# A hybrid pooling and window-attention layer: the MLP of three blocks as seven half-size products

## The reference

```python
n = rmsnorm(x)
h = x + (sig(gp) * pool(n) + sig(ga) * (attn(n) @ w_attn_up)) @ w_out   # the mixer
h = h + square(relu(rmsnorm(h) @ w_up)) @ w_down                        # the MLP, width 4096
y = rmsnorm(h)
```

## Time and profile before

| | |
|---|---|
| time, median of 3 runs | 2447.85 us (2447.26 to 2447.87) |
| span of the profiled execution | 2446.3 us |
| PE busy | 2423.0 us, 99% |
| DVE busy | 1328.5 us, 54% |
| ACT busy | 789.8 us, 32% |
| POOL busy | 173.1 us, 7% |
| DMA | 237.20 MB, 97 GB/s over the span |

### The profile page before, as it was taken

The page is one execution under the profiler, slowest core; times in us unless marked ns, Lnnn a source line. Parts: engine busy times, 40 slices in busy tenths (PEclk is TensorE's granted clock), DMA queues, the critical chain, the costliest instruction groups (busy, mean ns, idle before and its releaser), DMA issues.

```text
span 2446.3 us, 32439 instructions
## 1 busy us (share of the span) xinstructions
PE 2423.0 (99%) x12933; PEld 2055.9 (84%) x12933; DVE 1328.5 (54%) x1712; ACT 789.8 (32%) x1258; POOL 173.1 (7%) x168
## 2 busy tenths in 40 slices
PE   8999999999999999999999999999999999999997
PEld 8999999999977888888887788888887788888885
DVE  7645644445675564543576556445467555544444
ACT  4533322222443332222335334222243434222222
POOL 1400000000131000000024000000003400000000
PEclk9999999999999999999999999999999999999998
DMA  4223332222232333333332233332334233333231
GB/s 164 75 77 99 118 92 87 86 86 88 90 126 71 105 127 95 95 94 94 95 129 75 84 109 125 94 95 93 94 94 131 63 94 103 95 95 94 94 94 61
DMA packets 72248, 237.20 MB, mean 97 GB/s; under 512 B 8784, under 2 KB 9136, under 8 KB 72144
## 3 DMA queue, kind: packets, MB, share of 16 engines
q1 hardware_dynamic: 67408, 227.00, 30.0%
q10 hardware_dynamic: 4736, 8.75, 0.9%
HBM read 226.97 MB, written 8.85 MB: 96 GB/s over the span
## 4 chain that ended last, share of the span: by engine, by line
PE 99%; DVE 0%; DMA 0%; ACT 0%; DVEq 0%; issue 0%; SPq 0%; ACTq 0%
PE prod L335 95%; PE auxB L335 1%; PE auxA L439 1%; PE auxB L470 1%; PE auxB L453 1%; PE auxA L335 0%; DVE hT L774 0%; DMA raw<-weights 0%; DVE acc L756 0%; PE auxA L409 0%; DVE wL L728 0%; ACT wH L527 0%; DVE nL L762 0%; DVE acc L750 0%; DVE hT L944 0%; ACT acc L554 0%
## 5 line engine op out<-in xcount | busy, mean ns | idle before, releaser
L527 ACT ACTIVATE wH<-raw 128x1024 fp32r<-128x1024 f32 (+1 forms) x424 | 439.4, 1036 | 1530.3 <-PE prod L335 1526.7
L335 PE MATMUL prod<-nH,wH 128*128 128x512 f32 (+1 forms) x2320 | 747.1, 355 | 8.2 <-DVE nL L762 8.2
L335 PE MATMUL prod<-nL,wH 128*128 128x512 f32 (+1 forms) x2320 | 741.6, 352 | 0.0
L335 PE MATMUL prod<-nH,wL 128*128 128x512 f32 (+1 forms) x2320 | 741.4, 352 | 0.0
L728 DVE TENSOR_TENSOR wL<-raw,wH 128x1024 fp32r<-128x1024 f32 (+1 forms) x424 | 520.2, 1227 | 96.7 <-ACT wH L527 96.0
L335 PE MATMUL prod<-midL,wH 128*128 128x512 f32 (+1 forms) x1600 | 511.1, 352 | 0.0
L335 PE MATMUL prod<-midH,wL 128*128 128x512 f32 (+1 forms) x1600 | 511.1, 352 | 0.0
L335 PE MATMUL prod<-midH,wH 128*128 128x512 f32 (+1 forms) x1600 | 510.9, 352 | 0.0
L335 PEld LDWEIGHTS prod<-nH,wH 128*128 128x128 f32 x2320 | 407.9, 188 | 76.6 <-DVE wL L728 8.4
L335 PEld LDWEIGHTS prod<-nL,wH 128*128 128x128 f32 x2320 | 407.8, 188 | 61.2 <-issue 1.2
L335 PEld LDWEIGHTS prod<-nH,wL 128*128 128x128 f32 x2320 | 406.5, 188 | 60.6
(11 more groups left out here) (118 smaller groups left out, 1352.1 us busy)
## 6 DMA issues: line engine op xcount, KB each, us to landing
raw<-weights SPq DMA_DIRECT2D x392, 512.0 KB, 3.5
raw<-weights SPq DMA_DIRECT2D x32, 320.0 KB, 2.9
xT<-x SPq DMA_DIRECT2D x3, 2048.0 KB, 8.2
y<-hT ACTq DMA_DIRECT2D x12, 512.0 KB, 2.8
xT<-x SPq DMA_DIRECT2D x8, 272.0 KB, 5.3
y<-hT ACTq DMA_DIRECT2D x4, 544.0 KB, 2.8
rope<-tables SPq DMA_DIRECT2D x4, 512.0 KB, 4.4
cst<-consts SPq DMA_DIRECT2D x1, 96.0 KB, 6.6
```

The lines of the kernel that those rows point to most:

```text
L335: ins = nc.tensor.matmul(out[:, s, 0:hi - lo], lhs, rhs[:, lo:hi], start=first, stop=last)
L527: return nc.scalar.activation(out, in_, ACT.Copy, scale=scale)
```

## The change

Block 0 computes its MLP as before, but with two changes to who does what. In blocks 1 to 3 each product of the MLP is split in halves in its three dimensions (two halves of the tokens, of 256; two of the inputs, two of the outputs), and the 2x2x2 half-size block products, eight, are replaced by seven of sums of halves (one Strassen level in Winograd's form). A "token" in the code below is one such half-size product of one pair of output tiles `j` (tile j and tile j + 4) and one of seven kinds `r`: 4 input tiles, 3 matmuls each, of 256 columns, so 12 matmuls. A phase (an up or a down of one quarter) is 28 tokens, in the order of the table `ORDER`, and a block has 8 phases. The seven sums of the weights (four need arithmetic, three are the halves themselves) don't depend on the block. They are made in block 0 and kept in DRAM.

- **Block 0, new work.** For each of 32 pairs of units, POOL makes four 128x512 sums (`sum_weights`). In 5 of the 8 groups (`SPLIT_PHASES`; 20 pairs) ACT and DVE split three of the four sums (`sums_high`, `sums_low`, 128x1536 each), and SP stores 0.26 MB and 1.57 MB; in the others SP stores 1.05 MB. A place in `raw` is now also held until POOL has summed it, and POOL waits, before it writes one of two sets `wsum`, until the set's store has landed. ACT, not DVE, squares the hidden values now.
- **Blocks 1 to 3.** SP loads one half unit (0.26 MB) for a token, or a presplit sum (0.52 MB, high and low), which ACT and DVE needn't split. The hidden half blocks are put together from partial products by ACT copies, DVE additions and accumulation in PSUM (`up_step`); the down products are added to `hT` one by one (`down_step`), where they were added once per unit. The seven sums of the activations, too, are made and split by DVE and ACT (`gain_pair` in the mixer's last stage, `sum_T13` to `low2` in the MLP).

```diff
-                tt(work[:, 2, 0:n], work[:, m % 2, 0:n], work[:, m % 2, 0:n], ALU.mult).then_inc(hid_sq, 1)
+                    nc.scalar.activation(y, y, ACT.Square).then_inc(hid_sq, 1)
...
+ORDER = [(0, 1), (0, 5), (1, 1), (1, 5), (0, 2), (1, 2), (0, 6), (0, 3), (1, 6), (1, 3), (0, 7), (1, 7), (2, 5), (0, 4),
+         (2, 2), (1, 4), (2, 1), (3, 5), (3, 1), (3, 2), (2, 6), (2, 3), (3, 6), (3, 3), (2, 7), (3, 7), (2, 4), (3, 4)]
+SPLIT_PHASES = (0, 2, 4, 6, 7)
+def presplit(ph, pr):
+    return ph in SPLIT_PHASES and pr in (5, 6, 7)
...
+            def raw_place_free(*item):
+                for before in raw_free[item]:
+                    wait_split_low(sp, *before)
+                    if before[0] == "plain":
+                        wait(sp, s_S, before[2] // 2)
...
+            for n in range(2 * KD * NQ):
+                load_plain_unit(n)
...
+                if n % 2 and n >= 7:
+                    store_sums((n - 7) // 2)
...
+            def sum_weights(p):
...
+                if p >= 2:
+                    pool.wait_ge(set_out[p % 2], set_count[p - 2])
+                s = wsum[p % 2]
...
+                link(tt(s[:, 2, :], a11, a21, ALU.subtract))
+                link(tt(s[:, 1, :], s[:, 2, :], a22, ALU.subtract))
+                tt(s[:, 0, :], s[:, 1, :], a11, ALU.subtract)
+                tt(s[:, 3, :], a12, s[:, 1, :], ALU.add).then_inc(s_S.sem, 1)
...
+            def phase(b, ph):
+                every = (0, 1, 2, 3)
+                if ph % 2:
+                    for k in range(6):
+                        token(b, ph, k, (0, 1))
+                    for k in range(6):
+                        token(b, ph, k, (2, 3))
...
+                for kp in kps:
+                    if ph == 0 and k in (0, 4):
+                        wait(pe, s_gL2 if k == 0 else s_gL5, b, kp)
+                    if down and k in (0, 4):
+                        wait(pe, s_L5 if k == 0 else s_L2, b, q, kp)
+                    wh, wl = (wring[:, ring_slot(b, t), h, kp * P:(kp + 1) * P] for h in range(2))
+                    xh, xl = high[:, QUAD[r], kp, :], low[:, QUAD[r], kp, :]
+                    nc.tensor.matmul(out, wh, xh, start=kp == 0 and r in (1, 2, 5), stop=False, skip_group_check=True)
+                    nc.tensor.matmul(out, wh, xl, start=False, stop=False, skip_group_check=True)
+                    ins = nc.tensor.matmul(out, wl, xh, start=False, stop=kp == PAIRS - 1, skip_group_check=True)
...
+            def up_step(b, q, k):
+                if q == 0 and k == 6:
+                    invert("h", b)
+                    wait(dve, s_r, "h", b)
+                if k == 7:
+                    add_cb(b, q, 0)
+                    weights_ahead(b, 2 * q * NT7 + k)
+                    relu_z01(b, q, 0)
+                    return
...
+                if k in (10, 11):
+                    add_u3(b, q, k - 10)
+                    weights_ahead(b, 2 * q * NT7 + k)
+                    relu_z2(b, q, k - 10)
+                    return
...
+                if k == 27:
+                    sum_T13(b, q, 3)
+                    relu_z3(b, q, 3)
+                    sum_T2(b, q, 3)
+                    low5(b, q, 2)
+                    sum_T4(b, q, 2)
+                    low5(b, q, 3)
+                    sum_T4(b, q, 3)
+                    low2(b, q, 2)
+                    low2(b, q, 3)
+                weights_ahead(b, 2 * q * NT7 + k)
```

More of the change, by code:

```diff
@@ new lines, in build @@
+        rms, acc = own("rms", [P, CMAX]), own("acc", [P, CMAX])
+        kT = own("kT", [P, 2 * K_HALF + DEC])
+        vB = own("vB", [P, NT + 1, P])
+        cst = own("cst", [P, P + G * 16])
+        ones = own("ones", [P, P])
+        vec = own("vec", [P, 4 * KD + 6])
+        nsink = own("nsink", [P, 6])
+        eps_tile = own("eps", [P, 1])
+        columns = own("columns", [P, 7, 4])
+        carry, carry_s, state = (own(n, [P, G, 16]) for n in ("carry", "carry_s", "state"))
+        assert top[0] <= 229344
@@ L238, in wait @@
             eng.wait_ge(signal.sem, signal.count[item])
-        def unit_width(u):
-            return AO_WIDTH if u < M_MLP and MIXER[u][0] == "ao" else WIDTH
-        def wait_product(eng, b, i):
[L245 to L261, removed]
+        splits = []
@@ new lines, in raw_tokens, with ring_slot, wait_split_low, wait_raw @@
+        def raw_tokens(b, lo, hi):
+            return [t for t in range(lo, hi) if t < TOKENS and not is_split(b, t)]
+        def ring_slot(b, t):
+            return (t + SHIFT[b]) % RING
+        def wait_split_low(eng, *item):
+            eng.wait_ge(w_low, split_no[item])
+        def wait_raw(eng, *item):
+            eng.wait_ge(raw_in[raw_at[item]], raw_count[item])
+        def unit_width(i):
+            return AO_WIDTH if MIXER[i][0] == "ao" else WIDTH
+        def unit_row(b, i):
+            return MIXER.index(PLAN[b][i])
@@ L336, in stream, with three @@
                 return ins
-            def three(out, b, uslot, off, high, low, k, first, last):
-                wh, wl = wH[:, uslot, off:off + P], wL[:, uslot, off:off + P]
+            def three(out, b, wslot, off, high, low, k, first, last):
+                wh, wl = wslot[:, 0, off:off + P], wslot[:, 1, off:off + P]
                 stream(out, b, wh, high[:, k, :], first, False)
@@ L389, in before @@
                         sum_squares("f", b - 1)
-                product(b, i % 2, high, low, nk, before)
+                product(b, i, high, low, nk, before)
             def sum_squares(kind, b):
@@ L519, in _ @@
                     between(b, i)
-                quarters(pe, b, up, down, lambda b: down(b, NQ - 1))
+                if b == 0:
+                    for q in range(NQ):
+                        plain_up(q)
+                        plain_down(q)
+                else:
+                    for ph in range(PHASES):
+                        phase(b, ph)
             sum_squares("f", NB - 1)
@@ L621, in step @@
                     merged_high(b, m)
[L622 removed]
+                if kind == "out" and b == 0:
                     wait(act, s_h, b, m)
@@ new lines, in plain_down @@
+            def plain_down(q):
+                for i in range(KD):
+                    n = 16 * q + KD + i
+                    wait_plain(act, n)
+                    plain_split_ahead(n + 2)
+                    if q == NQ - 1:
+                        m = ORD[i]
+                        gained_high("x", 1, i)
+                        if i == 0:
+                            root("x", 1)
+                        act.wait_ge(down_added, hid(q, i))
+                        square("f", 0, i, hT)
+                        wait(act, s_sq, "f", 0, i)
+                        copy(hT[:, m, :], hT[:, m, :], g_fin[:, m:m + 1]).then_inc(s_fg.sem, 1)
+                    sums_high(n)
```

963 lines of the change are left out of this document (751 added, 212 removed).

## The result

| | before | after |
|---|---|---|
| time, median | 2447.86 us (2447.26 to 2447.99, 4 runs) | 2518.34 us (2515.88 to 2519.5, 4 runs) |
| span of the profiled execution | 2446.3 us | 2515.7 us |
| mean granted clock | 0.997 | 0.981 |

The ratio is 1.0286, with a 95% interval of 1.0273 to 1.0299: slower by 70.5 us, where 18 us less were forecast, and 38 us above the range. The page of after, beside the earlier trace rows: span and engines, the chain that ended last by engine and line, and the stores with their us to landing.

A forecast was written before the change was run, and what follows sets the result against it. PE was taken as the bound, without stalls at full clock: 2446.3 - 117.2 + 15.6 + 5.7 + 10.8 + 1.8 + 1.0 + 64.6 = 2428.6 us of span, so a median of 2430 us, range 2358 to 2480.

The forecast's parts named there:

- Ring: Block 0's MLP: POOL's sums, loads and stores wait in a circle, 15.4 and 13.2 us a pair against 12.02; +64.6 us.
- transfers: Loads and stores part of block 0's circle: 9.0 us in presplit pairs, 7.1 us in the others.
- second rival: Block 0: POOL and DVE block each other in each operation, eating the gain; 2482 to 2526 us; chance 0.22.
- Columns: MLP of blocks 1 to 3: 2688 matmuls of 256 columns at 118.15 ns replace 1536 at 232.21; -117.2 us.
- Weight load as a floor: Rival, blocks 1 to 3: 256 columns cost 125.28 ns like 272; 2476 us, or 2412 if block 0 keeps pace; chance 0.08.
- Turns: Up to down, 12 times: PE waits for DVE's relu (0.6 us) and `low5` (0.4), 1.3 us each; +15.6 us.
- Mixer to MLP: Join in blocks 1 to 3: token 4's weight split comes 1.9 us late behind DVE's sums, three times; +5.7 us.
- DVE at 90%: Up phases of blocks 1 to 3: DVE stays under PE's 39.7 us, at 90% or more, its work bunched.
- First and last quarter, handover: Reciprocal and root delay sums: +10.8 us in first quarters, +1.8 in last; handover to block 1 and end squares +1.0.
- the ring fits: Rival: loads and stores overlap, a pair stays under 12.02 us, block 0 keeps its length; 2366 us; chance 0.25.

The follow-up runs named there:

- experiment 2: Changed kernel with one more POOL subtraction in each of block 0's 32 pairs: 2560.33 us, +42.0 against the changed kernel.
- experiments 12 to 18: Seven runs on the kernel with earlier stores and both order changes (2377.25 us), shifting operand addresses or repeating weights: 2367.22 to 2377.09 us.
- experiment 9: Kernel before, each 512-column product of blocks 1 to 3 made as two of 256, first half's three instructions before the second's: 2481.50 us, +33.4.
- experiment 6: On top of experiment 1, `gain_low5` one product later, behind the next weight split, and ACT's high weights ahead of the gained halves: 2395.44 us, -20.2.
- experiment 5: On top of experiment 1, DVE makes `sum_T4` of pair 1 before `low5` in blocks 1 to 3: 2396.52 us, -19.1.
- experiment 1: Changed kernel with block 0's sums stored two weight loads earlier: 2415.66 us, 102.7 under the changed kernel, ratio to before 0.9869.
- 7 and 18: 7: experiment 5 and experiment 6 changes together on experiment 1, 2377.25 us. 18: 7 with weights placed 128 bytes higher against the moving columns, 2369.65 us.

## Why the prediction was wrong, step by step

- **Ring: the step that failed.** Its shape was right: loads that wait for sum p + 1, stores behind them, sum p + 2 behind the stores, with PE, ACT and DVE waiting in the order foreseen. Opening it gives 102.7 us back and lengthening it costs its full time. The size was 64.6. The term "transfers", 9.0 and 7.1 us, was too short: from the last sum to POOL's next start it took 11.3 us behind a store in two parts and 9.1 behind the others, on average. In the chain above it is 10.7 to the landing (407.7 to 418.4). SP's issues of 0.3 to 0.4 us each stand one after the other ahead of the store, and the DMA engines moved 184, 274, 209 and 293 GB/s in the four us from 409, where the forecast had 410 throughout, and only then 418 to 469. Why the first four were slow is not shown. POOL was priced too high, 6.4 and 6.1 for 5.7 and 5.3 us, which hid some of it. So the pairs came out at 17.0 and 14.4 us, for 15.4 and 13.2. Over 29 pairs POOL's starts are 15.9 us apart, 3.9 over PE's pace, or 113 us; forecast were 72 (17 x 3.4 + 12 x 1.2). About 10 us were taken by slack, near the 7.6 foreseen. The point of the second rival, 0.6 us a pair more than forecast, was passed. But its reason, POOL and DVE blocking each other in each operation, is not what passed it: POOL's operations had medians of 1.28 to 1.29 us in experiment 2's ring. The disturbance that the forecast priced shows where it costs little, in the first two pairs of the ring (8.0 and 7.0 us) and with the ring open (6.8 us a pair).
- **Clock.** Not in the prediction: beside waits of 2.2 to 6.1 us PE's clock fell. In the ring this cost nothing by itself (experiment 2), so a sum over the ring needed no term for it, while one over PE's waits does.
- **Columns.** -117.2 forecast. 8064 x 120.0 against 4608 x 232.21 ns is -102.3, 15 us short. The interpolated 118.15 was right for the width (118.34 measured). What it left out belongs to the changed kernel, and experiments 12 to 18 tie it to where the operands lie: the rows that it was drawn through, belong to tensors that lie otherwise. How the place acts stays open.
- **Weight load as a floor.** Excluded by experiment 9. The prediction doubted the Trainium skill's section "Identifying the Most-Contended Engine" ("Perfetto Trace Analysis") here, and the runs bear that out: full cover of the rows of weight loads at 272 columns did not mean that a narrower matmul couldn't start sooner.
- **Turns.** +15.6 forecast, 4.6 measured by starts (0.38 a turn, the first of the two waits; the second, for `low5`, didn't come). Priced between starts and busy times, DVE was taken as slower than it was: in block 1 the relu of the fourth pair was done 1.5 us behind the end of the last up token (1214.19 to 1215.71) for the 1.8 forecast.
- **Mixer to MLP.** +5.7 forecast, 20.2 by experiment 6. The 1.9 us at token 4 came (2.0 in the trace). Missed were, in block 1, the first token's split (0.8), the low part of the gained sums behind it (1.15) and the two waits inside the mixer's last stage (2.4), where ACT and DVE stand in each other's order. I had walked only the last product, not the seven before it.
- **Up phases.** Nothing forecast beyond the turns, 19.1 us by experiment 5: the copies at token 18 and 19 stand in ACT's order behind `high2` of another pair. "DVE at 90%" was named and then checked only at the ends of the phase.
- **First and last quarter, handover.** +10.8 forecast, 3 x 3.3 measured by starts; +1.8 forecast, 2 x 0.75. Of block 0's +6 us in experiment 1 only +1.0 was forecast. Some 2.5 us a block lie in breaks under 0.25 us and were not looked into.

Sum of what was measured: 2446.3 - 102.3 + 102.7 + 6.1 + 4.6 + 20.2 + 19.1 + 9.9 + 1.5 = 2508.1. The 7.6 us left to the 2515.7 of the trace are about what the small breaks come to. The rival "the ring fits" (2366) would have missed as well: with the ring open and nothing else changed the time is 2415.7, 50 us more, for the columns (15), the waits at the mixer, in the up phases and at the turns (21 net over the forecast), the small breaks (8) and block 0 (5). That 7 and 18, at 2377 and 2370, come near 2366 is no confirmation of it: they removed waits that it hadn't in it.

## What to carry to other kernels

When a buffer's release hangs on a second engine, write down the circle (who waits for whom, through which in-order queue) and its period as a sum, issue times and queueing behind the loads ahead included; then ask first whether a store can be issued before the loads that don't need it. That order was worth 103 us here, as much as the narrower products had taken away from TensorE. Where a helper engine is 90% busy, walk every step of the phase in both engines' orders, not only its ends. And follow a named wait one engine further back: the instruction it names may be waiting in order for a third one.

## What the runs showed of the hardware

- The granted clock went from full to half (2.4 to 1.2 GHz) 15 times from 265 to 790 us in the changed kernel, beside breaks of TensorE of 2.2 to 6.1 us, 2.2 to 5.2 us after the break began, and came back 2.8 to 5.9 us after work had begun again. Breaks of 2.0 us (at 382.8) and 2.3 us (at 632.5) left it at full. At half, matmuls of 272 columns began every 0.227 us, at full every 0.125.
- 256 columns of fp32r, each with a weight load: 118.34 ns from start to start, but 120.0 ns in five kernels where weights and columns lay at the same offset within 256 bytes, and 118.6 to 119.0 where they were 128 bytes apart. At 96 bytes it was 117.3 to 118.7, one phase excepted (120.0), but 512 columns took 0.9% longer. 128 free bytes brought 7.6 us in this kernel.
- A store of 1536 KB landed 6.1 us after its issue when it went alone, 9.5 us when two loads of 512 KB and a store of 256 KB were issued just ahead of it.
